# Attention scores issued by kind of operand, with value and query evacuations divided differently between VectorE and ScalarE

## The reference, cut to what matters

```python
def apply_rope(x, cos, sin):
    x1, x2 = x[..., :half], x[..., half:]
    return jnp.concatenate([x1 * c - x2 * s, x1 * s + x2 * c], axis=-1)

q = jnp.einsum('bsr,rhd->bshd', rmsnorm(u @ w_dq), w_uq)     # 16 heads, 128 + 64
s = (jnp.einsum('bqhd,bkhd->bhqk', q_nope, k_nope)
     + jnp.einsum('bqhr,bkr->bhqk', q_rope, k_rope)) * scale
p = softmax(where(key_pos <= q_pos, s, -inf))
o = jnp.einsum('bhqk,bkhd->bqhd', p, v) @ w_o
```

## Time and profile before

| what | value |
|---|---|
| median of 3 runs (lowest to highest) | 2347.74 us (2346.78 to 2347.82) |
| the profiled execution | 2345.91 us |
| its span, first to last instruction | 2344.0 us |
| mean granted TensorE clock | 0.996 |
| PE busy, DVE, ACT, POOL | 98%, 71%, 44%, 36% |
| chain that ended last | PE 84%, POOL 5%, DVE 5%, issue 2%, ACT 2%, DMA 2% |

### The profile page before, as it was taken

One profiled execution on the slowest core, in us unless ns is written; L12 is line 12 of the kernel. 1 busy time (PEld: TensorE's weight loads), 2 busy tenths in 40 slices (PEclk: granted clock), 3 DMA queues, 4 the chain that ended last, 5 costly groups with the idle time before them and its releaser, 6 DMA issues.

```text
span 2344.0 us, 33535 instructions
## 1 busy us (share of the span) xinstructions
PE 2308.6 (98%) x13510; PEld 2016.7 (86%) x13510; DVE 1665.8 (71%) x1672; ACT 1020.1 (44%) x1294; POOL 841.4 (36%) x441
## 2 busy tenths in 40 slices
PE   9999999999999999999999999999989999999998
PEld 7888788888789999979899879899967778899997
DVE  6687687772489678668587769696777743686874
ACT  5324443432355344554354454353444443453443
POOL 1321222121046446349256228356310001474561
PEclk9999999999999999999999999999999999999999
DMA  5221232332323333323342333332332222233322
GB/s 176 72 72 55 73 111 93 100 96 95 97 73 118 99 111 95 102 73 103 113 126 73 91 117 98 102 122 93 91 77 50 62 73 90 90 101 112 113 86 86
DMA packets 221332, 221.39 MB, mean 94 GB/s; under 512 B 11154, under 2 KB 217617, under 8 KB 221201
## 3 DMA queue, kind: packets, MB, share of 16 engines
q1 hardware_dynamic: 221040, 219.46, 29.8%
q10 hardware_dynamic: 160, 0.07, 0.0%
HBM read 213.22 MB, written 2.10 MB: 92 GB/s over the span
## 4 chain that ended last, share of the span: by engine, by line
PE 84%; POOL 5%; DVE 5%; issue 2%; ACT 2%; DMA 2%; SPq 0%; DVEq 0%; ACTq 0%; POOLq 0%
PE bank L1385 15%; PE bank L1387 15%; PE bank L1386 15%; PE bank L1379 10%; PE bank L1381 10%; PE bank L1380 10%; POOL sums L697 2%; POOL raw L698 1%; PE bank L2078 1%; PE bank L1514 1%; POOL sums L700 1%; PE bank L2027 1%; POOL sums L702 1%; PE bank L2030 1%; PE bank L2061 1%
## 5 line engine op out<-in xcount | busy, mean ns | idle before, releaser
L1379 PE MATMUL bank<-Xhi,wlo 128*128 128x256 f32 (+1 forms) x1283 | 374.2, 292 | 4.3 <-DVE Xlo L2382 2.8
L1380 PE MATMUL bank<-Xlo,whi 128*128 128x256 f32 (+1 forms) x1283 | 373.0, 291 | 0.0
L1381 PE MATMUL bank<-Xhi,whi 128*128 128x256 f32 (+1 forms) x1283 | 372.9, 291 | 0.0
L697 POOL TENSOR_TENSOR sums<-raw 128x512 f32<-128x512 f32 x72 | 147.2, 2044 | 430.5 <-DMA raw<-in_ffn_post_wg_dram 162.5
L1060 ACT ACTIVATE whi<-raw 128x2048 fp32r<-128x2048 f32 x72 | 138.3, 1921 | 370.5 <-PE bank L1387 230.7
L1379 PE MATMUL bank<-Xhi,sxlo 128*128 128x256 f32 (+1 forms) x960 | 281.0, 293 | 0.4 <-ACT kept L1099 0.2
L1380 PE MATMUL bank<-Xlo,sxhi 128*128 128x256 f32 (+1 forms) x960 | 278.9, 291 | 0.0
L1381 PE MATMUL bank<-Xhi,sxhi 128*128 128x256 f32 (+1 forms) x960 | 278.8, 290 | 0.0
L1379 PEld LDWEIGHTS bank<-Xhi,wlo 128*128 128x128 f32 x1283 | 241.8, 188 | 11.7 <-issue 4.5
L1380 PEld LDWEIGHTS bank<-Xlo,whi 128*128 128x128 f32 x1283 | 241.7, 188 | 6.5 <-issue 0.5
L1381 PEld LDWEIGHTS bank<-Xhi,whi 128*128 128x128 f32 x1283 | 241.8, 188 | 5.8
(11 more groups left out here) (389 smaller groups left out, 5597.4 us busy)
## 6 DMA issues: line engine op xcount, KB each, us to landing
raw<-in_ffn_w_up_dram SPq DMA_DIRECT2D x22, 1024.0 KB, 5.1
raw<-in_ffn_pre_wg_dram SPq DMA_DIRECT2D x22, 1024.0 KB, 5.3
raw<-in_ffn_pre_wu_dram SPq DMA_DIRECT2D x22, 1024.0 KB, 5.4
raw<-in_ffn_post_wg_dram SPq DMA_DIRECT2D x22, 1024.0 KB, 5.4
raw<-in_ffn_post_wu_dram SPq DMA_DIRECT2D x22, 1024.0 KB, 5.4
raw<-in_ffn_pre_wd_dram SPq DMA_DIRECT2D x24, 768.0 KB, 4.8
raw<-in_ffn_post_wd_dram SPq DMA_DIRECT2D x24, 768.0 KB, 4.8
raw<-in_w_in_dram SPq DMA_DIRECT2D x13, 1024.0 KB, 5.0
```

The lines of the kernel that those rows point to most:

```text
L697: nc.gpsimd.tensor_tensor(s1, a21, a22, ALU.add).then_inc(adds_done[h], 1)
L1379: nc.tensor.matmul(bank, wl, x, start=first, stop=False, skip_group_check=True)
L1380: nc.tensor.matmul(bank, w, xl, start=False, stop=False, skip_group_check=True)
L1381: return nc.tensor.matmul(bank, w, x, start=False, stop=last, skip_group_check=True)
```

## The change

- PE: a head's scores are issued as all fp32 matmuls, then all masks, then (after the wait for `rope_moved`, for even heads) all rotary matmuls; `scores_ready` is signalled by the second rotary matmul of a chunk. The fourth query group (n = 13) moves behind the scores of head 0.
- ACT: at the head of `attend` it copies value banks 6 and 7, counted by a new semaphore `values_act`, for which PE waits before the first transposes. Before quarter 0, ACT issues two of the four turning DMAs.
- DVE: it takes two value banks (8, 9) in place of four, and ahead of the wait for the turned queries. Then it rotates and evacuates by turns, and takes group 13 between the maxima and the normalisation of head 0. The sign flip of the sines moves behind the cosine products.

```diff
+            a.wait_ge(evacuated, GB["attn"] + 6)
+            for b in (2, 3):
+                src, dst = slice(b * 32, b * 32 + 32), slice((b ^ 1) * 32, (b ^ 1) * 32 + 32)
+                nc.scalar.dma_start(QRs[dst, :], QRr[src, :]).then_inc(qrope_turned, 16)
             def attend(q):
+                for n in (6, 7):
+                    a.wait_ge(groups_done, q * 14 + (GB["attn"] + n + 1))
+                    nc.scalar.activation(tile(VV, n - 6), banks[n][:, :], ACT.Copy).then_inc(values_act, 1)
                 rope_queries_hi(q)
...
-                for x in range(4):
+                for x in range(3):
                     queries(x, 10 + x)
...
-                        for key in rope_key:
-                            nc.tensor.matmul(ring[i][:, 0:n], rope_two[h][:, i * P:(i + 1) * P], key[:, 0:n],
-                                             start=False, stop=False)
-                        nc.tensor.matmul(ring[i][:, i * P:n], identb[:, :], causal[:, :],
+                    for i in range(i0, i1):
+                        nc.tensor.matmul(ring[i][:, i * P:(i + 1) * P], identb[:, :], causal[:, :],
+                                         start=False, stop=False)
+                    if h % 2 == 0:
+                        pe.wait_ge(rope_moved[h // 2], q * 32 + 32)
+                    for i in range(i0, i1):
+                        n = (i + 1) * P
+                        nc.tensor.matmul(ring[i][:, 0:n], rope_two[h][:, i * P:(i + 1) * P], rope_key[0][:, 0:n],
+                                         start=False, stop=False)
+                        nc.tensor.matmul(ring[i][:, 0:n], rope_two[h][:, i * P:(i + 1) * P], rope_key[1][:, 0:n],
                                          start=False, stop=True).then_inc(scores_ready, 1)
...
                 scores(0)
+                queries(3, 13)
...
+                        pe.wait_ge(values_act, q * 2 + 2)
...
+                def rotate(j):
                     nc.vector.tensor_tensor(tile(QRs, j), tile(QRs, j), rope_q[:, T:2 * T], ALU.mult
                                             ).then_inc(qrope_part, 1)
-                for j in range(2):
                     v.wait_ge(qrope_part, q * 4 + (j + 3))
                     nc.vector.tensor_tensor(tile(QRt, j), tile(QRt, j), tile(QRs, j), ALU.add
                                             ).then_inc(qrope_ready, 1)
...
+                take_values(8)
+                take_values(9)
+                v.wait_ge(qrope_turned, q * 64 + 64)
+                v.wait_ge(sin_signed, 2)
+                rotate(0)
+                take(10, tile(QN, 0))
+                rotate(1)
+                rope_queries_lo(q, 0)
+                take(11, tile(QN, 1))
+                rope_queries_lo(q, 1)
+                take(12, tile(QN, 2))
...
                 maxes(0)
+                take(13, tile(QN, 3))
                 normalise(0)
```

More of the change, by code:

```diff
@@ L371, in build @@
         rope_key_ready = sem("rope_key_ready")
+        values_act = sem("values_act")
         scores_ready = sem("scores_ready")
@@ L611, in quarter_weights, with turn_queries @@
                              heads(1, NOPE, NOPE + ROPE)).then_inc(raw_ready[1], 16)
-            def turn_queries(q, taken):
+            def turn_queries(q, taken, blocks=range(4)):
                 sp.wait_ge(evacuated, taken)
-                for b in range(4):
+                for b in blocks:
                     src, dst = slice(b * 32, b * 32 + 32), slice((b ^ 1) * 32, (b ^ 1) * 32 + 32)
@@ L632, in _ @@
             quarter_weights(1)
-            turn_queries(0, GB["attn"] + 6)
+            turn_queries(0, GB["attn"] + 6, (0, 1))
             join_halves(0)
@@ L2010, in attend @@
                           True, True).then_inc(groups_done, 1)
-                for x in range(4):
+                for x in range(3):
                     queries(x, 10 + x)
                 def scores(h, i0=0, i1=TC):
-                    if h % 2 == 0:
-                        pe.wait_ge(rope_moved[h // 2], q * 32 + 32)
                     for i in range(i0, i1):
@@ L2792, in _ @@
             gb = GB["attn"]
-            for b in (0, 2):
-                minus = rope_q[b * 32:b * 32 + 32, T:2 * T]
-                nc.vector.tensor_scalar(minus, minus, -1.0, None, ALU.mult).then_inc(sin_signed, 1)
             def take_keys(q, x, n):
@@ L2825, in _ @@
             rope_cosines(0, 4)
+            for b in (0, 2):
+                minus = rope_q[b * 32:b * 32 + 32, T:2 * T]
+                nc.vector.tensor_scalar(minus, minus, -1.0, None, ALU.mult).then_inc(sin_signed, 1)
             def attend(q):
@@ L2836, in take_values @@
                     v.wait_ge(groups_done, q * 14 + (gb + n + 1))
-                    nc.vector.tensor_copy(tile(VV, n - 6), banks[n % 8][:, :]).then_inc(evacuated, 1)
-                v.wait_ge(qrope_turned, q * 64 + 64)
-                v.wait_ge(sin_signed, 2)
-                for j in range(2):
+                    nc.vector.tensor_copy(tile(VV, n - 6), banks[n % 8][:, :]).then_inc(evacuated, 2)
+                def rotate(j):
                     nc.vector.tensor_tensor(tile(QRs, j), tile(QRs, j), rope_q[:, T:2 * T], ALU.mult
                                             ).then_inc(qrope_part, 1)
-                for j in range(2):
                     v.wait_ge(qrope_part, q * 4 + (j + 3))
```

## The result

The changed kernel takes 2356.26 us (median of 6 runs, 2354.39 to 2358.63), the kernel before 2347.78 us beside it (6 runs, 2346.78 to 2352.23): a ratio of 1.0035, 95% interval 1.0022 to 1.0048. It is slower, by 8.5 us.

What follows compares the result with a forecast made beforehand. PE, busy 98%, bounds the kernel with the chain feeding it, measured at head 0's normalisation. Terms -1.45 + 4.6 + 4.6 - 0.4 - 0.9 = +6.5 us on 2347.74 give 2354.2 us; 8 in 10 range 2349.0 to 2360.0.

Steps and rivals of the forecast that it cites:

- quarter 0: First attention quarter: two DMA queues give 1.8 us, queries turned at 1723.3 not 1725.94; head 0's normalisation ends 1.45 us earlier.
- quarter 1: Second attention quarter: head 0's normalisation ends at 1791.5 against 1786.83, +4.6 us, held by the split and by POOL.
- quarter 2: Third attention quarter: repeats quarter 1, +4.6 us.
- last quarter: Attention quarter without a split: head 0's normalisation ends 0.4 us earlier by the same chain.
- behind it: Remainder of the attention stage following the last quarter: -0.2 us forecast.
- The step that decides: ACT's split waits for the later group 13, head 0's exponentials queue behind it; PE idles some 2.8 us.
- POOL's hold: Head 0's normalisation on DVE waits for POOL's half of the split, ending 1.26 us after POOL (upper bound taken).
- The clock: Rival: PE's granted clock also falls behind the new idle in three quarters, +3.3 us, 2357.5 us; chance 0.15.
- Order by kind: PE's scores in heads 2 and 3: saved weight loads, some 0.25 us a quarter, -0.9 us in all.
- Normalisation not held by POOL: Rival: DVE normalises head 0 while POOL works; sum -0.5 us, 2347.2 us, no change; chance 0.19 with smaller mixtures.
- The split hidden after all: Rival: ACT's split does not hold head 0's exponentials; sum -10.1 us, 2337.6 us, faster; chance 0.06.
- ACT's value copies: Value bank copies on ACT fall in time when it waits for the rotation, and cost nothing.

Runs made afterwards that it cites:

- e1: Changed kernel with ACT's wait for group 13 and split of the next weights moved behind head 0's exponentials; 2337.59 us, 0.9962 of the kernel before.
- e2: Changed kernel with the fourth query group back ahead of head 0's scores on PE; 2340.35 us, 0.997 of the kernel before.
- e3: Changed kernel with POOL's half of the split waiting for head 0's normalisation; 2350.81 us, 1.0012 of the kernel before.
- e4: Changed kernel with all four turning DMAs of quarter 0 on SP and none on ACT; measured once, 2353.89 us.
- e6: e3 with 11 filler matmuls in each of the first three quarters, while PE waits for the exponentials; 2347.1 us, 1.0002 of the kernel before.
- e5: e2 with the old order of a head's scores and the old place of the wait for the rotary halves; 2353.43 us, 1.0026 of the kernel before.
- e11: e1 with the scores of heads 1 to 3 chunk by chunk again, only head 0 by kind; 2339.32 us, 0.996 of the kernel before.
- e9: Kernel before with only the scores ordered by kind and the rotary wait moved behind the masks; 2347.56 us, 1.0003 of the kernel before.
- e7: e1 with the fourth query group between masks and rotary wait, and all turning DMAs on SP; 2340.45 us, 0.9974 of the kernel before.

## Why the prediction was right, and where its terms were off

Slower was forecast, at 2354.2 us, and 2356.26 was measured, inside the range. By the steps, with the end of head 0's normalisation placed in the stage (its start in the table plus its length), each quarter measured from the one before it:

| step | forecast | measured |
|---|---|---|
| quarter 0 | -1.45 | -0.33 |
| quarter 1 (+4.6, less a quarter of the order's 0.9) | +4.4 | +4.39 |
| quarter 2 | +4.4 | +4.44 |
| last quarter | -0.6 | +0.63 |
| behind it | -0.2 | 0.0 |
| stage | +6.5 | +9.14 |

- **The step that decides** held to 0.1 us in quarters 1 and 2, and not because errors cancelled. Behind quarter 0's normalisation, quarter 1's rotation starts at 31.01 us (31.15 forecast), the rotary matmuls at 37.87 (38.0), the split at 40.98 (41.0), and POOL ends at 47.55 (47.6). The split loses its cover, ACT's exponentials queue behind it, and PE idles (2.49 us; I had some 2.8). e1 and e2 each take this one link away, from ACT's side and from PE's, and the kernel is faster than before.
- **POOL's hold.** I took the upper bound, a normalisation that waits for POOL's end, and 1.26 us from there to its own. It ends 1.08, 1.07 and 1.07 us after POOL, the first of its four instructions after 2.46 us and 0.10 behind POOL, and e3 shows the cause: with POOL held back it lasts 1.27 us. That is the rule of the Trainium skill, SBUF — State Buffer, section "SBUF: two separate sides", and the trace now agrees with it for this operation, where the earlier trace rows only let one infer it from another stage.
- **Quarter 0** is the mis-sized term. The 1.8 us for two DMAs on each queue came out at 0.3: 4.64 us from first issue to rotation against 4.93, and less than the spread of the other profiles. So the rotation starts 1.3 us earlier in the stage than before (8.76 in place of 10.07), where I had 2.6. I had reckoned with the issue of the last DMA alone. The issue does not bind: in e4, four on one queue in 2.52 us are ready no later. Why a DMA lands later with two queues stays open.
- **The clock** was a rival at 0.15, and it is part of the truth. It falls in all three quarters behind the new idle. I argued that this would mostly be covered by the wait for POOL and DVE, which is so in quarters 0 and 1; in quarter 2 it falls later and costs 1.66 us up to head 1's normalisation (9.23 us from head 0's in place of 7.57), of which 1.13 are left at the end of the quarter (46.48 less 45.35 of e4). That is nearly all of the last quarter's miss. The Trainium skill's rule that idle between bursts puts the engine back to its lower clock (TensorE: Matmul & The Clock Gate, on HAM oscillation) agrees with the windows of after, e3 and e6, although the waits of that section's example are longer than these; but e4 and e5 each have a stretch of 2.49 and 2.24 us of idle with 1.00 behind it, so it does not happen every time.
- **Order by kind.** Its -0.9 in the later heads was about right: e11 gives back 0.76 in the three distances. The working behind it was not sound: no row shows 0.05 us for a weight load, and eight chunks of it would be 0.4 us a quarter, not 0.25. Its main worth lies in head 0, where the sum counted the fp32 matmuls as done before the halves landed without giving this a price: with the old order it would be some 12 us more (e5).
- **Normalisation not held by POOL** did not occur, as the 3.44 us show. **The split hidden after all** did not either; e1 makes it occur. That its price, 2337.6 us, is e1's time of 2337.59 is luck: the price was -10.1 us of stage, and e1's stage gains 7.95. Up to the end of quarter 0's normalisation it gains 5.5 where the price had 7.0, and the 1.5 between them are the turned queries again, which reach DVE 1.1 us earlier in the stage in place of 2.6.
- **ACT's value copies** cost nothing, as forecast: in e1, which has them, only 0.5 us of PE's waits in the stage are put down to ACT.

## What to carry to other kernels

When a matmul group is moved later, follow every wait on its count, and then read what stands behind that wait in the waiting engine's queue: here a change that could save 9.6 us (e1) lost 8.5 because four exponentials stood behind a 1.9 us split that waits for the moved group. Take the pieces of such a change apart in both directions, since two halves that are each worth nothing or less (e5, e9) may be worth 6 us as a pair. And an idle stretch on PE should be priced twice, once for itself and once for the clock behind it, whose cost depends on whether other work covers the next few us. Before two single traces are subtracted, look for the part that varies by itself, here the turning DMAs: twice it made up a fifth or more of a difference that the edit seemed to explain (e3 to e6, e1 to e7).

## What the runs showed that I had not expected

- Added matmuls made the stage shorter: 11 of them in each of three waits of 2.5 us kept the clock at 1.00 in place of 0.53 to 0.57, and 2.9 of the 3.8 us from e3 to e6 are theirs.
- Whether the clock falls behind the same idle changes from quarter to quarter of one execution: in e5, behind 2.20, 2.24 and 2.22 us of idle, it was 0.66, 1.00 and 0.60 in the next 4 us. In e11 it fell behind 0.97 us of idle in quarter 0, where e1 and after kept 1.00 behind the same wait. What decides this stays open.
- Four DMAs issued from two queues instead of one were not ready clearly sooner (4.28 to 5.77 us on two, 4.47 to 5.38 on one). The spread of 1.5 us is as large as some of the effects that were being measured. Where it comes from is open.
